# Latent attention turned from a chain of row-wide programs into one program on heads, with its input norms moved into the sparse attention's program

## The reference, cut to what matters

```python
def mla_attention(c_q, c_kv, k_rope, ...):
    cos, sin = rope_tables(s, 64)
    q = (rms_norm_2(c_q, cq_gain) @ w_uq).reshape(b, s, 4, 128 + 64)
    kv = (rms_norm_2(c_kv, ckv_gain) @ w_ukv).reshape(b, s, 4, 128 + 128)
    q_nope = rms_norm_2(q[..., :128], qn_gain)
    q_rope = apply_rope_2(rms_norm_2(q[..., 128:], qr_gain), cos, sin)
    k_nope = rms_norm_2(kv[..., :128], kn_gain)
    v = kv[..., 128:]
    k_r = apply_rope_2(rms_norm_2(k_rope, kr_gain), cos, sin)   # one for all heads
    q_full, k_full = concat(q_nope, q_rope), concat(k_nope, k_r)
    return causal_attention(q_full, k_full, v, 192 ** -0.5)     # 4 heads
```

## Time and profile before

| | us |
|---|---|
| median of 3 runs (2633.11 to 2635.43) | 2635.41 |
| the profiled execution | 2635.67 |
| its span in the profile | 2633.9 |
| TensorE busy in the span | 2396.4 (91%) |
| DVE busy | 1770.4 (67%) |
| ACT busy | 1320.5 (50%) |
| mean granted clock of TensorE | 0.942 |

### The profile page before, as it was taken

One profiled execution on the slowest core, in us unless ns is written; L12 is line 12 of the kernel. 1 busy time (PEld: TensorE's weight loads), 2 busy tenths in 40 slices (PEclk: granted clock), 3 DMA queues, 4 the chain that ended last, 5 costly groups with the idle time before them and its releaser, 6 DMA issues. The chain is left out here.

```text
span 2633.9 us, 44570 instructions
## 1 busy us (share of the span) xinstructions
PE 2396.4 (91%) x17195; PEld 2175.7 (83%) x17195; DVE 1770.4 (67%) x2860; ACT 1320.5 (50%) x2068; POOL 186.5 (7%) x171
## 2 busy tenths in 40 slices
PE   7898999889988989979789987488999999999998
PEld 5787898679878779979689987377999999999997
DVE  3555555555555555565755556657999999999997
ACT  2343433433443534442444432135778777777776
POOL 0500000000005000008100012100000000000000
PEclk9899999989998989989799987778999999999999
DMA  8524555155633044534045541025999999999995
GB/s 342 196 96 176 192 216 201 64 208 216 234 131 139 6 176 173 188 124 160 1 155 183 190 182 49 0 89 209 343 340 342 334 342 338 336 344 332 337 346 214
DMA packets 82228, 542.86 MB, mean 206 GB/s; under 512 B 9328, under 2 KB 9840, under 8 KB 33904
## 3 DMA queue, kind: packets, MB, share of 16 engines
q1 hardware_dynamic: 79184, 529.57, 54.3%
q10 hardware_dynamic: 2848, 10.55, 1.1%
HBM read 539.03 MB, written 1.05 MB: 205 GB/s over the span
## 5 line engine op out<-in xcount | busy, mean ns | idle before, releaser
L847 PE MATMUL bank<-w_hi,src_hi 128*128 128x256 f32 x2304 | 664.0, 288 | 16.2 <-DVE src_lo L618 6.7
L3017 DVE TENSOR_TENSOR w_lo<-ring,w_hi 128x1024 fp32r<-128x1024 f32 x528 | 637.3, 1223 | 46.1 <-ACT w_hi L2946 33.7
L848 PE MATMUL bank<-w_lo,src_hi 128*128 128x256 f32 x2304 | 656.4, 285 | 0.0
L849 PE MATMUL bank<-w_hi,src_lo 128*128 128x256 f32 x2304 | 654.9, 284 | 0.0
L847 PEld LDWEIGHTS bank<-w_hi,src_hi 128*128 128x128 f32 x2304 | 444.8, 193 | 35.2 <-issue 25.0
L848 PEld LDWEIGHTS bank<-w_lo,src_hi 128*128 128x128 f32 x2304 | 445.3, 193 | 6.8
L849 PEld LDWEIGHTS bank<-w_hi,src_lo 128*128 128x128 f32 x2304 | 446.0, 194 | 0.0
L847 PE MATMUL bank<-src_hi,w_hi 128*128 128x256 f32 x1472 | 426.4, 290 | 13.1 <-DVE w_lo L1177 8.9
L1177 DVE TENSOR_TENSOR w_lo<-ring,w_hi 128x1024 fp32r<-128x1024 f32 x264 | 322.9, 1223 | 168.9 <-ACT w_hi L1114 168.8
L848 PE MATMUL bank<-src_lo,w_hi 128*128 128x256 f32 x1472 | 421.6, 286 | 0.0
L849 PE MATMUL bank<-src_hi,w_lo 128*128 128x256 f32 x1472 | 421.4, 286 | 0.0
(11 more groups left out here) (421 smaller groups left out, 2794.5 us busy)
## 6 DMA issues: line engine op xcount, KB each, us to landing
ring<-in_moe SPq DMA_DIRECT2D x176, 1024.0 KB, 7.2
ring<-in_ffn SPq DMA_DIRECT2D x66, 1536.0 KB, 6.6
ring<-in_moe SPq DMA_DIRECT2D x176, 512.0 KB, 6.8
ring<-in_ffn_ev SPq DMA_DIRECT2D x22, 1536.0 KB, 6.5
oT<-in_w_ada SPq DMA_DIRECT2D x20, 1024.0 KB, 5.5
big<-in_w_ada SPq DMA_DIRECT2D x20, 1024.0 KB, 8.3
ring<-in_w_in SPq DMA_DIRECT2D x18, 1024.0 KB, 6.4
ring<-in_w_out SPq DMA_DIRECT2D x12, 1024.0 KB, 4.9
```

Source lines behind the costliest of these rows:

```text
L847: pe.matmul(out, ah, bh, start=start and i == 0, stop=False, skip_group_check=True)
L848: pe.matmul(out, ah, bl, start=False, stop=False, skip_group_check=True)
L849: mm = pe.matmul(out, al, bh, start=False, stop=stop and i == n - 1, skip_group_check=True)
L3017: dve.tensor_tensor(wl, piece, wh.bitcast(F32), ALU.subtract).then_inc(p.w_lo[kind].sem, 1)
```

## The change

- `mla`'s three input norms and kr's rope become `mla_norms`, called in `nsa`'s DVE list between keeping turned column 6 and `activate(0)`. It takes one root for all three (6 columns) instead of three, and multiplies by root and gain in one instruction per tile and part. It also copies kr beside itself (columns 1752 to 1816), so that one turned tile has it in both halves. POOL's list in `nsa` gets `rsqrts(p, pool, [6])` ahead of the one it had.
- The other five programs of `mla` become one. ACT squares the up projections straight from PSUM; DVE sums; POOL takes one root of 12 columns per tile. The root is applied on the way out of PSUM: by DVE for queries and their rope parts, by ACT for keys. The rope parts are held as two heads side by side, so that 2 transposed pairs (one per pair of heads) take the place of 4. The gains of queries and keys (`mla_cols`, two new columns of the small inputs) are applied as a scale per partition when the turned heads leave PSUM. Attention runs by heads (4) instead of items (8): both query tiles' scores lie in one bank, the mask is added on the two diagonal blocks only, in PSUM, and one copy keeps the head's three turned probability blocks.
- Each engine's list is written out by hand; `jobs` is the order of turned tiles.

```diff
 # nsa, POOL
+            rsqrts(p, pool, [6])
             rsqrts(p, pool, [2], parts=N_CMP)
 # nsa, DVE
             for j in (4, 6):
                 keep_turned(j)
+            mla_norms(p, chain, dve)
             activate(0)
+def mla_norms(p, chain, dve):
+    proj, junk = p.proj, p.work[:]
+    parts = ((1304, 256, "cq"), (1560, 128, "ckv"), (1688, 64, "kr"))
+    st = p.small[:, 0:6]
+    for i, (a, n, _) in enumerate(parts):
+        square_sums(p, chain, dve, heads_of(proj, a, 1, n), junk[:, 2 * (a - 1304):], st[:, 2 * i:2 * i + 2])
+    for i, (a, n, _) in enumerate(parts):
+        v = st[:, 2 * i:2 * i + 2]
+        ins = dve.tensor_scalar(v, v, 1.0 / n, EPS, ALU.mult, ALU.add)
+        if i < 2:
+            chain(ins)
+    ins.then_inc(p.meansq.sem, 1)
+    rsqrt(p, dve, st)
+    for i, (a, n, name) in enumerate(parts):
+        for t in range(NT):
+            v = proj[:, t, a:a + n]
+            ins = dve.scalar_tensor_tensor(out=v, in0=v, scalar=st[:, 2 * i + t:2 * i + t + 1], in1=p.row(ROWS2, name),
+                                           op0=ALU.mult, op1=ALU.mult)
+    chain(ins)
+    rope_rows(chain, dve, heads_of(proj, 1688, 1), p.con_at(CON2, "rope_c", NT), p.con_at(CON2, "rope_s", NT), junk)
+    chain(dve.tensor_copy(proj[:, :, 1752:1816], proj[:, :, 1688:1752]))
 # mla: the new order on TensorE
+    jobs = [("q", 0), ("k", 0), ("r", 0), ("q", 1), ("k", 1), ("q", 2), ("k", 2), ("r", 1), ("q", 3), ("k", 3)]
...
+            pe.wait_ge(*up_freed_a(4))
+            pe.wait_ge(*up_freed_v(4))
+            for j in range(3):
+                turn_job(j)
+            score(0)
+            for j in (3, 4):
+                turn_job(j)
+            score(1)
+            turn_probs(0)
+            for j in (5, 6, 7):
+                turn_job(j)
+            score(2)
+            values(0)
+            turn_probs(1)
+            for j in (8, 9):
+                turn_job(j)
+            score(3)
+            values(1)
+            turn_probs(2)
+            values(2)
+            turn_probs(3)
+            values(3)
 # mla: DVE
+            keep_low(0)
+            keep_low(2)
+            squares(0)
+            squares(1)
+            for t in range(NT):
+                keep_queries(t)
+                rotate(t)
+            for j in (1, 2):
+                keep_turned(j)
+            maxima(0)
+            keep_turned(4)
+            maxima(1)
...
 # mla: ACT
+            keep_low(1)
+            keep_low(3)
+            squares(0)
+            squares(1)
+            for t in range(NT):
+                keep_values(t)
+            keep_turned(0)
+            keep_turned(3)
+            exps(0)
+            keep_turned(5)
+            keep_probs(0)
+            exps(1)
...
```

More of the change, by code:

```diff
@@ L482, in rsqrts @@
         pool.tensor_tensor(v, v, p.neg_half[0:parts, 0:w], ALU.pow).then_inc(p.rstd.sem, 1)
[L485 to L492, removed]
 def norm_rows(p, chain, eng, src, gains, junk, on_pool=False):
@@ L1345, in attention @@
     sunk.passed(sinks(n))
[L1348 to L1356, removed]
 def pool_chain(p, pool):
@@ L2590, in _ @@
             chain = Chain(dve, p.sig("dve_chain"))
[L2591 to L2648, removed]
@@ new lines, in keep_queries @@
+            def keep_queries(t):
+                dve.wait_ge(*rooted(t + 1))
+                for c in range(2):
+                    hs = slice(2 * c, 2 * c + 2)
+                    dve.tensor_tensor(q[:, t, hs, 0:P], pair(t, c)[:, :, 0:P],
+                                      st[:, t, 0, hs].unsqueeze(2).broadcast_to([P, 2, P]), ALU.mult)
+                    chain(dve.tensor_tensor(q_turn(t)[:, c, :].rearrange("p (h d) -> p h d", h=2), pair(t, c)[:, :, P:192],
+                                            st[:, t, 2, hs].unsqueeze(2).broadcast_to([P, 2, HD]), ALU.mult))
+                    dve.sem_inc(up_freed_v.sem, 1)
@@ new lines, in maxima @@
+            def maxima(u):
+                dve.wait_ge(*scores(u + 1))
+                s = p.ps[u % 2]
+                dve.tensor_tensor(s[:, 0:P], s[:, 0:P], edge, ALU.add)
+                chain(dve.tensor_tensor(s[:, 2 * P:3 * P], s[:, 2 * P:3 * P], edge, ALU.add))
+                for t in range(NT):
+                    ins = dve.tensor_reduce(att(u)[:, t:t + 1], s[:, AT[t]:AT[t + 1]], AX_X, ALU.max)
+                chain(ins)
+                dve.tensor_scalar(att(u)[:, 0:2], att(u)[:, 0:2], -scale, None, ALU.mult).then_inc(negmax.sem, 1)
@@ new lines, in _ @@
+            for j in (1, 2):
[3 more added lines that the diff above has]
+            maxima(1)
+            for j in (6, 7):
+                keep_turned(j)
+            maxima(2)
+            keep_turned(9)
+            outs(0)
+            maxima(3)
+            for u in (1, 2, 3):
+                outs(u)
+    for s, k in ((low_turned, 4), (low_kept_a, 2), (low_kept_v, 2), (up, 8), (up_freed_a, 4), (up_freed_v, 4),
+                 (squared, 8), (meaned, NT), (rooted, NT), (rotated, NT), (turned, len(jobs)), (kept_a, 4), (kept_v, 6),
+                 (scores, 4), (negmax, 4), (probs, 8), (pt_ready, 4), (pt_kept, 4), (pv, 4), (done, 4)):
+        s.passed(k)
```

213 lines of the change are left out of this document (198 added, 15 removed).

## The result

The changed kernel takes **2617.5 us** (median of 4, 2616.06 to 2622.23) where the kernel before takes 2634.3 beside it (2630.47 to 2635.43): a ratio of 0.9944, 95% interval 0.9928 to 0.9959. It is faster, and outside the range: 16.8 us were saved where 27.2 were forecast, and the forecast had 2616.0 as its upper end. The profiled execution took 2622.23. It is the slowest of the four, so its span, 13.4 us shorter than before, shows a little less of the gain than the medians.

What follows compares the result with a forecast made beforehand. TensorE was taken to bound the launch, with DVE chains in the norms and a low clock in attention. 1.9 + 0.5 + 21.9 + 24.0 + 0.4 = 48.7 for 75.85 us, 27.2 less: 2608.3, range 2601 to 2616.

Steps and rivals of the forecast that it cites:

- Part 1: Input norms moved into NSA: 7.9 us of DVE work, partly hidden in idle time; NSA 1.9 us longer, bounds 0 to 4.
- NSA longer by over 4: Sign that the forecast is wrong: the NSA program grows by more than 4 us.
- Part 2: Front of the new `mla` program: first score starts 21.9 us after its first transpose, where it was 52.3.
- Part 3: Heads of `mla`: 26.3 us all at the low clock, 24.0 with a clock rise, 16 if high throughout.
- 5.2 of waits over 8 items: Old attention: 84 records, 17.9 us of its 23.11, the remaining 5.2 taken as waits.
- halfway: Heads of `mla`: the clock rises midway, saving 2.3 us, 26.3 to 24.0.
- high everywhere, 2600: End of the high-clock rival: heads of `mla` at the high clock throughout, total 2600 us; rival's chance 0.20.
- Low clock throughout the heads: Rival: heads of `mla` stay at 1.2 GHz, taking 26.3 us, total 2610.6; chance 0.30.
- POOL stretching DVE: Rival: POOL's work slows DVE products in moved norms, front and heads; up to 2668 us, chance 0.03.
- No table load was added: ScalarE in `mla`: alternating Square, Exp, Copy and Identity adds nothing; by the skill, a switch and back would cost 5.3 us.
- The end moved whole: Against the no-gain rival, where MoE's weight loads fix the end at 2637 us; chance 0.02.
- The rule of the Trainium skill: Transposes don't engage the full clock, so they would lend the heads nothing: total 2610.6 us; the earlier trace disagreed.

Runs made afterwards that it cites:

- the two pairs that take it away: Moved norms placed before the copies of turned columns 4 and 6, against the changed kernel: 2615.49 us; both with five extra matmuls in `mla`: 2612.11 against 2618.36.
- its shifted twin: Changed kernel with NSA's first transpose 1.45 us later, behind two unused DVE products: 2622.85 us, ratio 0.9948 to the kernel before.
- the last kernel: Changed kernel with norms earlier, heads' tiles turned one score earlier and five unused 512-column matmuls before the first turned tile: 2600.94 us, ratio 0.9861.
- the gap alone: Kernel before with eleven unused DVE products (7.9 us) ahead of `activate(0)` in NSA: 2637.03 us, ratio 1.0014.
- the shift: Kernel before with NSA's first transpose 1.45 us later, behind two unused DVE products: 2647.36 us, ratio 1.0039.
- the matmul in NSA: Kernel before with one unused 512-column matmul behind NSA's second score: 2633.60 us, ratio 1.0003.
- the fourth job: Changed kernel with norms earlier and heads' tiles turned one score earlier: 2612.32 us; the same with five extra matmuls before the first turned tile: 2600.94.

## Why the prediction was wrong, step by step

**Part 1, the step that failed: "NSA gets 1.9 us longer".** The duration of the norms (8.0), the wait behind `activate(0)` and the delay of `compressed(0)` came as worked out. The step priced the insertion by the gap alone and took the rest of NSA as it stood in the profile, clock and all. NSA's heads run for some 40 us, partly at either level, and how much of them is low moves with everything ahead: 74.2 in the changed kernel, 62.3 and 66.3 with the same gap at two other shifts, 66.2 with the gap in the kernel before; and without a gap 60.2 (before, and twice more), 66.0 (three times), 64.2 to 65.5 with one matmul more (three times), and 69.1 after a shift of 1.45. The kernel before stood at the best end of these: its 60.2 was the lowest length seen, so in these profiles an edit ahead of it could only lose. The bounds of the step, 0 to 4, were about DVE's products; the term that spreads over 14 us had none. Of the forecast's excess of 14.6 (63.3 measured for 48.7), 12.1 is this. By the repeated runs the gap costs less than the one profile says: 5.5 and 6.3 in the two pairs that take it away. The last sentence of the prediction did name it as a sign of error ("NSA longer by over 4").

Why the clock stays at 0.50 with TensorE busy all of 1640 to 1656 in one kernel and rises at once in its shifted twin is open. The runs show that it depends on alignment as well as on the gap: at the changed kernel's own place the rise came 50.6 us after the first transpose with the gap, and 29.9 to 30.1 without it (the three profiles of 66.0). Of the runs without a profile only the mean clock over the launch is known, not where it was low.

**Part 2, the front: right.** 21.9 forecast, 20.9 measured; the 1.0 lies in the up projections (last product over at 11.3, forecast 12.3); roots of 12 columns 2.27 each (forecast 2.3), beside DVE's work with no product stretched (`keep_queries` at 0.42 and 0.28). The boundary took 0.4.

**Part 3, the heads: 24.0 forecast, 28.0 measured; a term was mis-sized.** All at the low clock they cost 32.3, not 26.3. The step that failed is "TensorE's work in records of 128 columns ... 0.213": it gives a score 2.56 us (12 times 0.213) by a rate taken from transposes, and a score took 3.72, so the sum has 4 x 1.16 = 4.6 too little. The values took 1.44 for 1.28 a head (0.6 in all). The waits, from start to start less the work between, were 1.08, 0.92 and 1.15 before the scores, 0.8 twice before values and 1.27 at the end: 6.0 for 5.4 forecast. 26.3 + 4.6 + 0.6 + 0.6 = 32.1. The old attention could have told it. Its timeline, kernel before:

```profile
1728.84 1.36 PE L1265 MATMUL bank<-big 128*128 128x128 f32 x4
1730.13 0.69 PE L1273 MATMUL bank<-ident,work 128*128 128x128 f32 x2
1730.61 0.63 PE L1283 MATMUL bank<-projc,work 128*128 128x128 f32 x2
1731.04 2.21 PE L1265 MATMUL bank<-big 128*128 128x256 f32 x4
1733.18 0.48 PE L1273 MATMUL bank<-ident,work 128*128 128x128 f32 x1
```

A head's two score groups go from 1728.84 to 1730.13 and from 1731.04 to 1733.18, 3.43 together, and no bracket stands behind any line. The earlier trace rows itself has TensorE busy 21.39 of the 23.11, so at most 1.7 idle: most of what the prediction took for "5.2 of waits over 8 items" was matmul time. It had priced the old attention by a rate that belonged to another operation, and called the remainder idle. The same misreading hid that the new heads (28.0, at a mean clock of 0.64) are hardly shorter than the old turn and attention, 6.4 + 23.1 = 29.5 at 0.55 to 0.60. Of the 26.5 won between NSA and the output projection, 25.0 lie ahead of the first score (the first four stretches of the earlier trace rows, 45.96, became 20.94), and the norms are what went there.

The clock's rise in the heads was forecast "halfway", to save 2.3. By the prediction's own ends (26.3 all low, 16 all high) a rise halfway saves 5.2 and gives 21.1, so the 2.3 doesn't follow, and its 24.0 is nearer to the measured 28.0 by luck. The rise saved 4.3 (32.3 less 28.0), though it came late, at 1723.4, for the last 8 us. The mechanism held in part. In the two profiles whose heads began at the high clock and had waits before the scores it fell; in the two without such waits or with them filled it stayed. But the order without waits did not raise a low clock for 17 us. And "high everywhere, 2600" is what the last kernel reached, by edits that the change hasn't got.

**The rivals.** Low clock throughout the heads happened in four of the edited kernels, but at 32, not 26.3. POOL stretching DVE did not happen. No table load was added: the trace has none in `mla`, with Square, Exp, Copy and Identity in one list. The end moved whole. The rule of the Trainium skill (TensorE: Matmul & The Clock Gate, Part 4) on transposes can be held against three more traces, those of the edited kernels before (the gap alone, the shift, the matmul in NSA). There TensorE waits 22.2 us, then runs nothing but the transposes of L818, and as they end the clock goes from 0.50 to 1.00 (at 1726.0, 1730.6 and 1725.8, where they began at 1720.5, 1725.5 and 1719.9), ahead of the attention's first matmul. These three traces disagree with the rule as the earlier trace rows does. **The chance** of faster (0.95) was right; the range was too narrow because the clock was a term in the heads and nowhere else.

## What to carry to other kernels

When an edit stands ahead of a stretch that runs at both clock levels, price that stretch at either level and keep the difference in the range: here an insertion worked out to a tenth of a microsecond cost 5 to 14 with what came after (5.5 and 6.3 by the repeated runs, 14.0 in the profile). Take a matmul's price from start to start of the same operation on the same shapes, and call time a wait only where the trace shows one. In this program an order without waits and extra matmuls ahead of it belonged together: each alone gave 0.1% to 0.2%, about the noise, the two together 0.5%, with some part of it from NSA's alignment. And one profile of a kernel is one place against the clock's changes: compare stretches of the same instructions over several profiles before a cause is named.

## What the runs showed of the hardware that was not expected

- A delay of 1.45 us in one DVE list, in the kernel before, cost 11.8 us of a 2635 us launch (1.0039, 1.0023 to 1.0056), eight times itself.
- TensorE without an idle moment for 16 us (four windows of 4.00 of 4.00) was held at 1.2 GHz, and ran at 2.4 GHz soon after in the same program.
- One and the same NSA program took 66.0 us in one kernel of the fourth job and 60.2 in the other, where it began 4.06 and 4.36 us after the clock's last fall.
- At the low clock an f32 matmul record of 128 columns took 0.35 us from start to start in the scores (0.69 for two), 0.24 in the values (1.44 for six), and a transposing one 0.213. At the high clock a score took 2.06 for 3.72, 0.55 of the low clock's time.
- The root by power on POOL took 1.34 us for 6 columns and 2.27 for 12, in line with the earlier trace rows at about 0.16 us a column.
